# Dense matmuls between the steps of a gated delta rule: laid at every second step instead of at each

## The reference

```python
    lower = jnp.where(strict, jnp.einsum('nbhid,nbhjd->nbhij', kb, k) * decay, 0.0)
    sol = lax.linalg.triangular_solve(eye + lower, rhs, left_side=True, lower=True)
    u, w = sol[..., :DV], sol[..., DV:]
    attn = jnp.einsum('nbhid,nbhjd->nbhij', q, k) * decay

    def step(S, xs):
        u_c, w_c, attn_c, qd_c, kd_c, gl_c = xs
        v_new = u_c - jnp.einsum('bhcd,bhde->bhce', w_c, S)
        o = jnp.einsum('bhcd,bhde->bhce', qd_c, S) + jnp.einsum('bhij,bhje->bhie', attn_c, v_new)
        S = S * gl_c[..., None, None] + jnp.einsum('bhcd,bhce->bhde', kd_c, v_new)
        return S, o
```

## Time and profile before

| | |
|---|---|
| median of 3 runs | 2250.95 us (2249.39 to 2251.83) |
| the profiled execution: its time, its span | 2249.54 us, 2246.9 us |
| PE busy over the span | 2168.1 us (96%) |
| PEld busy | 1714.1 us (76%) |
| DVE busy | 1071.0 us (48%) |
| ACT busy | 860.3 us (38%) |
| mean granted clock of PE | 0.984 |

### The profile page before, as it was taken

How to read it: one execution, slowest core, us unless ns; L and a number is a source line. 1 busy time by engine, 2 the same in 40 slices (tenths; PEclk the granted TensorE clock), 3 DMA queues, 4 the chain that set the end, 5 groups by cost and what they waited for, 6 DMA issues and landing times. The chain is left out here.

```text
span 2246.9 us, 32537 instructions
## 1 busy us (share of the span) xinstructions
PE 2168.1 (96%) x13696; PEld 1714.1 (76%) x13696; DVE 1071.0 (48%) x1642; ACT 860.3 (38%) x1402; POOL 86.4 (4%) x118
## 2 busy tenths in 40 slices
PE   8989999999999899999999999999999999999999
PEld 6757678888887897666989866678874578888887
DVE  4445756777633464444436634435431344444422
ACT  4325544444422463222515421236356623223211
POOL 0011310000000000000000000000012100000000
PEclk9999999999999999999999999999999999999999
DMA  4331012233322321110342110123200232332332
GB/s 169 104 103 47 1 40 91 95 94 94 99 98 85 113 76 48 39 48 29 113 132 85 57 57 30 38 67 114 85 20 1 75 122 88 99 95 94 94 94 94
DMA packets 51425, 175.80 MB, mean 78 GB/s; under 512 B 6480, under 2 KB 10960, under 8 KB 50640
## 3 DMA queue, kind: packets, MB, share of 16 engines
q1 hardware_dynamic: 51280, 173.72, 23.8%
HBM read 164.20 MB, written 8.45 MB: 77 GB/s over the span
## 5 line engine op out<-in xcount | busy, mean ns | idle before, releaser
L282 PE MATMUL ps<-nx_hi,whi 128*128 128x512 f32 (+3 forms) x1696 | 575.0, 339 | 13.0 <-PEq L2192 6.3
L283 PE MATMUL ps<-nx_lo,whi 128*128 128x512 f32 (+3 forms) x1696 | 572.0, 337 | 0.0
L284 PE MATMUL ps<-nx_hi,wlo 128*128 128x512 f32 (+3 forms) x1696 | 570.8, 337 | 0.0
L268 ACT ACTIVATE whi<-raw 128x1024 fp32r<-128x1024 f32 x282 | 297.4, 1055 | 591.4 <-PE ps L284 535.5
L277 DVE TENSOR_TENSOR wlo<-raw,whi 128x1024 fp32r<-128x1024 f32 x282 | 344.4, 1221 | 260.0 <-ACT whi L268 259.5
L282 PEld LDWEIGHTS ps<-nx_hi,whi 128*128 128x128 f32 x1696 | 321.9, 190 | 57.4 <-DVE wlo L277 7.2
L284 PEld LDWEIGHTS ps<-nx_hi,wlo 128*128 128x128 f32 x1696 | 322.1, 190 | 33.8
L283 PEld LDWEIGHTS ps<-nx_lo,whi 128*128 128x128 f32 x1696 | 321.6, 190 | 33.8
L282 PE MATMUL ps<-mixer_out,whi 128*128 128x512 f32 x384 | 154.2, 402 | 5.8 <-PEq L2764 3.8
L283 PE MATMUL ps<-mixer_out,whi 128*128 128x512 f32 x384 | 153.5, 400 | 0.0
L284 PE MATMUL ps<-mixer_out,wlo 128*128 128x512 f32 x384 | 153.3, 399 | 0.0
(11 more groups left out here) (437 smaller groups left out, 2907.5 us busy)
## 6 DMA issues: line engine op xcount, KB each, us to landing
raw<-stream_dram SPq DMA_DIRECT2D x285, 512.0 KB, 3.4
arena<-keys_dram SPq DMA_DIRECT2D x1, 2112.0 KB, 8.6
h_sb<-x_dram SPq DMA_DIRECT2D x4, 512.0 KB, 6.8
mixer_floats<-cmp_w_k_dram SPq DMA_DIRECT2D x8, 256.0 KB, 4.1
mixer_floats<-cmp_w_v_dram SPq DMA_DIRECT2D x8, 256.0 KB, 4.5
h_dram<-h_sb SPq DMA_DIRECT2D x1, 2048.0 KB, 8.3
gate_dram<-arena SPq DMA_DIRECT2D x1, 2048.0 KB, 8.4
keys_dram<-h_sb SPq DMA_DIRECT2D x1, 2048.0 KB, 9.2
```

Source lines behind the costliest of these rows:

```text
L268: act.activation(K.whi[:, n % HL], K.raw[:, n % RAW], ACT.Copy).then_inc(K.s_hi, 1)
L282: pe.matmul(out, whi, xhi, start=start, stop=False, skip_group_check=skip)
L283: pe.matmul(out, whi, xlo, start=False, stop=False, skip_group_check=skip)
L284: return pe.matmul(out, wlo, xhi, start=False, stop=stop, skip_group_check=skip)
```

## The change

The two tables get new weights. The sums (38 for the meta block, 67 for a block x) stay, so as many dense matmuls as before lie in each block; they lie at other points. Points with 4 become 0 or 8 in turn, and where the 8 stands it is ahead of the answer for which PE waits there. An empty line is added as well, so that lines from there on have a number higher by one.

```diff
-SIDE_META = {"ug": 4, "lower": 8, "a_sb": 4, "x2_sb": 4, "a4_sb": 4, "x8_sb": 4, "r_sb": 4, "u_sb": 6}
-SIDE_X = {"ug": 4, "lower": 12, "a_sb": 4, "x2_sb": 4, "a4_sb": 4, "x8_sb": 4, "r_sb": 4, "k_sb": 4, "k2_sb": 4, "y_sb": 4,
-          "w_sb": 4, "nw": 3, "vn 0": 4, "state 1": 4, "vn 1": 4}
+
+SIDE_META = {"ug": 4, "lower": 8, "a_sb": 0, "x2_sb": 8, "a4_sb": 0, "x8_sb": 8, "r_sb": 0, "u_sb": 10}
+SIDE_X = {"ug": 0, "lower": 16, "a_sb": 0, "x2_sb": 8, "a4_sb": 0, "x8_sb": 8, "r_sb": 0, "k_sb": 8, "k2_sb": 0, "y_sb": 8,
+          "w_sb": 0, "nw": 7, "vn 0": 0, "state 1": 8, "vn 1": 4}
 SIDE_POINTS = list(SIDE_META.items()) + TT * list(SIDE_X.items())
 SIDE_CHUNK = 3 * KT
```

## The result

The changed kernel takes 2301.93 us (median of 4 runs, 2292.90 to 2305.42), the kernel before 2251.26 us (4 runs, 2249.39 to 2251.83): a ratio of 1.022, 95% interval 1.0191 to 1.025. 2290 us was forecast, in 2277 to 2305.

A forecast was written before the change was run, and what follows sets the result against it. The prediction took PE to bound both delta_rule calls. It added 33 us of waits less seams and 6 us for the clock, +39 us on the median of 2250.95, giving 2290 us, range 2277 to 2305.

The forecast's parts named there:

- waits less seams: Both calls: bare waits at emptied points, less 0.20 us for each dense run saved: 33.2 us.
- the clock: Falls of PE's clock behind the long waits at block starts: 3 us a call, 6 in all; bounds 0 and 14.
- What bounds the part: Both delta_rule calls: PE busy 190.8 of 193.1 us, 2.3 us idle, nearly nothing to win by covering waits better.
- Seam and answer: Emptied points: a run of n takes 0.20 + 0.23 n us; bare ACT answer +0.34, a4_sb +0.73, r_sb +0.38 us.
- The weight loads: At PE's waits: loads stay behind the wait; if they went ahead, the sum would be 8 us lower.
- The openings: Four transitions a call into blocks x, where PE waits for DVE without dense work: together 8.3 us a call.
- One sign of being wrong: Outside the two calls: time moving by more than 2 us would show the prediction wrong.
- the one with swings of the clock: Rival: short waits let the clock fall mid-block, +13 us, 2303 us; with two falls a block 2316; chance 0.15.
- the one with shorter waits: Rival: no falls at new long waits, answers 0.1 us cheaper at some 40 points: 2280 to 2270 us; chance 0.12.
- That of seams alone: Rival: empty points cost nothing, 31 fewer dense runs a call give 12 us: 2239 us; chance 0.03.

The follow-up runs named there:

- the second (2293.60): The changed kernel itself measured and profiled once more, nothing altered: 2293.60 us against 2251.10 for the kernel before, ratio 1.0194.
- opening_only: Kernel before, with only ug 4 to 0 and lower 12 to 16 in the blocks x: 2262.58 us against 2249.12, ratio 1.0058.
- late_chunk: Kernel before, with only vn 0 from 4 to 0 and state 1 from 4 to 8: 2253.20 us against 2247.31, ratio 1.0031.
- the kernel with filled waits: Changed kernel plus 12 (at x = 3: 4) unread matmuls before the wait at each block's ug: 2281.74 us, ratio 1.0144 to the kernel before.
- inversion: Kernel before, with only points a_sb to nw of the blocks x changed as in the change: 2263.87 us against 2249.12, ratio 1.0055.
- meta block: Kernel before, with only the meta block's table changed as in the change: 2257.10 us against 2247.31, ratio 1.004.
- the kernel whose openings are filled with its own work: Kernel before, with vn 0 and vn 1 from 4 to 0 and ug from 4 to 12: 2239.09 us against 2247.31, ratio 0.9962.
- the kernel with waits of 1.9 us at its openings: Changed kernel, with ug back from 0 to 4 and lower from 16 to 12 in the blocks x: 2285.34 us, ratio 1.0157 to the kernel before.

## Why the prediction was right, and which term was too small

The forecast lay 12 us below the first median and 4 us below the second (2293.60). Its own sum was 33.2 us for waits less seams and 6 for the clock. The first profile shows 34.6 and 14.9, and 7.2 us outside the calls; the second 34.6, 3.5 and -0.1.

**What bounds the part.** Right: PE, with 2.3 us of idle time a call, none of which the table could win by alternating. That there was nearly nothing to win by covering waits better was too strong: moving cover from `vn 0` and `vn 1` to the openings won 5.9 us a call, 2.0 of them from PE's idle time.

**Seam and answer.** Right, but for 0.1 us at `a4_sb`. A dense run takes 0.20 + 0.23 n us also at nine and ten (2.29 and 2.50 to 2.53 us), and the price of an ACT answer was seen as 0.56 us (1.17 instead of 0.61 us for eight products and the wait), for 0.54 predicted. At `a4_sb` the 24 products and the wait take 2.57 us for 1.54 without it: 1.03 us, for 0.93 predicted. PE in block 0 of the changed kernel, `a4_sb` and then `k2_sb`:

```profile
919.13 1.61 PE L2244 MATMUL ps<-mixer_floats 64*64 64x64 f32 x48
921.70 1.15 PE L2244 MATMUL ps<-mixer_floats 64*64 64x64 f32 x32 [0.95 <-DVE mixer_floats L2357]
...
930.33 0.68 PE L2244 MATMUL ps<-mixer_floats 64*64 64x64 f32 x16
931.49 0.68 PE L2244 MATMUL ps<-mixer_floats 64*64 64x64 f32 x16 [0.48 <-ACT mixer_floats L2472]
932.10 0.50 PE L2147 MATMUL ps<-nx_lo,whi 128*128 128x512 f32 x1
```

`vn 0` was hidden, as read from the earlier trace rows.

**The weight loads.** Right by the row: with 3.24 us of waiting in front of it, PE was back 0.06 us after the end of L2386, no earlier than the 0.05 in the earlier trace rows. At the 27 waits of each call in the first profile the load starts at most 0.03 us ahead of its matmul and at least 0.05 us after the answer.

**The openings.** Right in each: 3.31 us from x = 0 to 1 and from 1 to 2, and 3.5 us behind the meta block (3.6 forecast), 3.45 of them idle. `opening_only` and `late_chunk` show the two halves apart: the lost cover, and the chunk's work that moved in front of L2386.

The waits less the seams were forecast at 16.6 us a call and measured at 17.3, by the kernel with filled waits. Nearly all of the difference is `a4_sb` and the 0.02 us at each ACT answer, 0.6 us a call.

**The clock: the term that was too small.** I took 3 us a call, with a fall of 3.3 us as the normal case. The first profile had 7.7 and 7.2 us. A stretch of 6.8 us at an opening costs more than 1.6 us: from L2275 to L2249 it took 8.96, 9.53 and 9.81 us in the blocks 0, 1 and 2, against 6.92 us in block 3, which had no fall. The cost is the smaller the more of the stretch lies in the wait itself, where PE does nothing (2.2, 1.0 and 0.3 us of it in these three). And the meta block has a fall of its own, 1.6 us. That one is not in the 7.7 us, since the kernel before had a fall of the same length at the opening of x = 1. But the second profile of the same program shows the other end: 212.1 us, 1.7 above the filled kernel. So this term is no constant: with falls at every opening it is over 7 us a call, with few of them below 2. The forecast's bounds for both calls, 0 and 14 us, held for the second profile (3.5) and were 0.9 us too low for the first (14.9); the mean of the two is 9.2, for 6 forecast. I had expected two or three falls a call: the first profile has four, the second two.

**One sign of being wrong was badly chosen.** The time outside the calls should not have moved by more than 2 us. In the first profile it did, by 7.2 us, and in the second by 0.1. Over the profiles of all these kernels, which are the same program there but for the line numbers, it lies between 1859.9 and 1867.9 us. So 2 us is within what separates two executions. Those 7 us, and not only the clock in the calls, carried the profiled run to 2305.42 us, just beyond the range; how much of them is in the first median, 2301.93 us, no other profile of that set can tell.

**Of the rivals**, the one with swings of the clock was right for the meta block and wrong for the blocks x. Of the one with shorter waits, the answers were no shorter, while the clock did stay up behind four of six long waits in the second profile. That of seams alone came to nothing.

The parts (inversion, openings, meta block, late chunk), by their profiles, come to 9.2 + 5.9 + 3.6 + 1.3 = 20 us a call, for 24.8 of the whole in the first profile and 19.1 in the second. Their sum is not exact, since lost cover and late chunks lengthen the same waits and each profile has its own falls of the clock. Left open: what decides, for one and the same wait, whether the clock falls.

## What to carry to other kernels

Filler work belongs where the wait is longer than it, in proportion to the answer's latency; where other products already hide the answer it covers nothing and costs its seam (here 0.20 us), and two neighbouring points don't lend each other cover. Before weights in such a table are moved, look at what else rides on their running sum: here DVE's evacuations moved with them to the worst places. A long idle stretch of PE can be paid twice, once as itself and once, in some runs, as the half-speed stretch behind it.

## What the runs showed of the hardware that I had not expected

The same wait of 3.2 us in the same program was followed by 0 or by 6.8 us of the clock's lower level, and in a neighbouring kernel by 3.4 us; a wait of 1.9 us by 0 or 3.4 us. The changed kernel's runs spread accordingly, by 12.5 us in its first set and 10.1 in its second, those of the kernel whose openings are filled with its own work by 3.5 us; but few runs stand behind each figure, and the kernel with waits of 1.9 us at its openings spread by only 2.4. 40 matmuls a call whose results nobody reads brought the changed kernel's median from 2301.93 and 2293.60 us to 2281.74. In the profiled executions the two calls together differ by 14.9 and 3.5 us, which is the clock's part. And a fall can come with hardly any idling: in the meta block it followed 16-row products with waits of 0.3 to 0.5 us.
